# A hybrid decoder step on one core: norm and row sum links placed between masked maxima, and a rotation in four operations

## The reference

```python
h = rms_norm(x, norm_g); p = h @ w_in          # 1024 -> 3328 columns
# group A: 8 query heads, 2 key/value heads of 64, window 128
qa, ka = rotary(rms_norm(q), pos, 16, 5e5), rotary(rms_norm(k), pos, 16, 5e5)
s = einsum(q, k) * 64 ** -0.5; m = max(max(s + mask), sink)
prob = exp(s - m) / (sum(exp(s - m)) + exp(sink - m)); A = prob @ v
# group B: 4 retention heads of 128 with a decayed state
x = x + concat(silu(g_A) * A, silu(g_B) * B) @ w_out
```

## Time and profile before

| | |
|---|---|
| profiled execution, own time | 2014.24 us |
| its span | 2012.4 us |
| granted TensorE clock, mean | 0.978 |
| TensorE busy | 1858.1 us, 92% |
| VectorE busy | 1442.5 us, 72% |
| ScalarE busy | 712.0 us, 35% |
| block A's steps from 2 on, layer 0 | 97.4 to 422.7 us |
| block A's steps from 2 on, layer 1 | 1108.7 to 1400.7 us |
| a step, layer 0, from `L943` to `L943` | 23.2 (4 to 6), 21.4 to 21.8 (7 to 11), 20.3 (12), 19.0 (13), 19.1 (14), 17.8 and 18.7 us |
| a step, layer 1 | 19.9 to 20.3 (3 to 5), 19.1 to 19.5 (6 to 14), 18.0 and 18.4 us |

### The profile page before, as it was taken

One profiled execution on the slowest core, in us unless ns is written; L12 is line 12 of the kernel. 1 busy time (PEld: TensorE's weight loads), 2 busy tenths in 40 slices (PEclk: granted clock), 3 DMA queues, 4 the chain that ended last, 5 costly groups with the idle time before them and its releaser, 6 DMA issues.

```text
span 2012.4 us, 36841 instructions
## 1 busy us (share of the span) xinstructions
PE 1858.1 (92%) x12264; PEld 1047.5 (52%) x12264; DVE 1442.5 (72%) x4918; ACT 712.0 (35%) x1841; POOL 68.5 (3%) x108
## 2 busy tenths in 40 slices
PE   1778999997999999978998999999999999999999
PEld 0445555553555555543444655555555555555444
DVE  6679899976665666677885899999666657666542
ACT  4444565541232213232442455555213221232110
POOL 3010000010000000021001000001000000000000
PEclk9899999998999999999999999999999999999999
DMA  8332222032000210079994000001210021003864
GB/s 245 67 120 53 58 52 53 16 130 83 11 11 10 98 61 11 11 152 264 242 244 135 8 16 16 10 16 57 78 51 10 10 97 62 11 10 92 225 202 143
DMA packets 203403, 163.03 MB, mean 81 GB/s; under 512 B 145073, under 2 KB 175985, under 8 KB 203153
## 3 DMA queue, kind: packets, MB, share of 16 engines
q1 hardware_dynamic: 193584, 126.33, 23.2%
q0 software_dynamic: 9728, 35.66, 5.4%
HBM read 88.75 MB, written 41.16 MB: 65 GB/s over the span
## 4 chain that ended last, share of the span: by engine, by line
PE 60%; DVE 21%; ACT 4%; issue 4%; DMA 2%; SPq 1%; DVEq 0%; ACTq 0%
PE PA L499 24%; PE PB L499 24%; DVE r L1003 3%; ACT r L1564 2%; DVE r L979 2%; DVE mix L1043 2%; PE S L646 2%; PE OB L665 2%; PE TK L635 1%; PE S L681 1%; PE OB L672 1%; PE X L598 1%; DVE w_mx L834 1%; DMA r<-r 1%; DMA out<-land 1%
## 5 line engine op out<-in xcount | busy, mean ns | idle before, releaser
L499 PE MATMUL PA<-w_a,hT 128*128 128x512 f16 (+1 forms) x1920 | 405.2, 362 | 13.2 <-DVE land L957 13.2
L499 PE MATMUL PB<-w_a,hT 128*128 128x512 f16 (+1 forms) x1920 | 405.2, 362 | 0.0
L499 PEld LDWEIGHTS PA<-w_a,hT 128*128 (+1 forms) x1920 | 186.2, 99 | 187.5 <-DVE land L957 14.1
L499 PEld LDWEIGHTS PB<-w_a,hT 128*128 (+1 forms) x1920 | 185.8, 99 | 180.5 <-issue 11.8
L499 PE MATMUL PA<-w_b,hT 128*128 128x512 f16 x768 | 182.5, 389 | 16.8 <-DVE land L957 16.8
L499 PE MATMUL PA<-w_b,r 128*128 128x512 f16 x768 | 174.4, 384 | 19.4 <-DMA r<-r 17.1
L1564 ACT ACTIVATE r<-r,nm,unqk 128x256 f32<-128x256 f32 x256 | 150.5, 589 | 109.9 <-DVE sd L1011 109.9
L499 PE MATMUL PB<-w_b,hT 128*128 128x512 f16 x768 | 176.3, 379 | 0.0
L1622 ACT ACTIVATE r<-OB 128x128 f32<-128x128 f32 (+1 forms) x136 | 36.3, 272 | 389.8 <-PE S L681 362.4
L499 PE MATMUL PB<-w_b,r 128*128 128x512 f16 x768 | 171.3, 379 | 0.0
L1092 DVE TENSOR_TENSOR r<-S,t_dec 128x256 f32<-128x256 f32 x64 | 27.2, 425 | 154.4 <-PE S L646 154.2
(11 more groups left out here) (247 smaller groups left out, 2784.0 us busy)
## 6 DMA issues: line engine op xcount, KB each, us to landing
out<-r SPq DMA_DIRECT2D x40, 512.0 KB, 4.7
r<-mixed SPq DMA_DIRECT2D x32, 512.0 KB, 4.1
r<-in_x_prompt SPq DMA_DIRECT2D x25, 512.0 KB, 4.3
w_b<-in_w_in POOLq DMA_DIRECT2D x16, 512.0 KB, 9.0
mixed<-mix SPq DMA_DIRECT2D x32, 256.0 KB, 2.0
w_a<-in_w_in POOLq DMA_DIRECT2D x16, 512.0 KB, 8.6
mixed<-mix SPq DMA_DIRECT2D x64, 128.0 KB, 1.8
w_b<-in_w_out POOLq DMA_DIRECT2D x16, 512.0 KB, 7.5
```

The lines of the kernel that those rows point to most:

```text
L499: last = nc.tensor.matmul(out[0:s.rows, 0:n], lhs, w16(ph, k, p, wpart), start=(k == 0 and part == 0 and wpart == 0), stop=(k == KT - 1 an ...
```

## The change

It concerns VectorE's program of block A. `Chain` gets `put` (raise the semaphore) and `wait` apart. Steps 3 to 16 of each layer take a new order, written out in `a_tile`: the three row sum links of (u, 1) stand between the maxima of (t, 0); the norm links of tile s and the row sum links of (t, 0) stand between the maxima of (t, 1), the two lo parts of the probabilities of (t, 0) and the lo parts of weights. Both lo parts of weights are ahead of the rotation. In all steps the rotation multiplies both halves of the 16 channels by cos in one operation and by sin in another. No other engine's program changes.

```diff
+    def put(self, ins):
+    def wait(self):
...
             def a_rotate(L, s, ch):
...
-                V.tensor_tensor(rp1[0:r, :, 0, :], xa, cos, ALU.mult)
-                V.tensor_tensor(rp1[0:r, :, 1, :], xb, cos, ALU.mult)
-                V.tensor_tensor(rp2[0:r, :, 0, :], xa, sin, ALU.mult)
-                ch(V.tensor_tensor(rp2[0:r, :, 1, :], xb, sin, ALU.mult))
+                both = x[:, :, 0:ROT].rearrange("p h (c d) -> p h c d", c=2)
...
+                V.tensor_tensor(rp1[0:r, :, :, :], both, cos, ALU.mult)
+                ch(V.tensor_tensor(rp2[0:r, :, :, :], both, sin, ALU.mult))
...
                 def a_step(s, k=None):
+                    if not (s.fixed and s.c < 3):
+                        a_tile(s, k)
+                        return
...
+                def a_tile(s, k):
+
+                    t, u = s - 1, s - 2
+                    a_lo(L, t)
+                    a_land_q(L, s)
+                    a_plo(L, u, 1)
+                    old = a_rr(L, u, 1)
+                    alone(v, a_s, 2 * an(L, t) + 1)
+                    sm = Chain(v, ch_asp, 2, 2 * tn(L, t))
+                    a_rr_link(u, 1, old, 0)
+                    a_mask(t, 0, 0)
+                    a_rr_link(u, 1, old, 1)
+                    a_mask(t, 0, 1)
+                    a_rr_link(u, 1, old, 2)
+                    a_mask(t, 0, 2)
+                    sm.put(a_mask(t, 0, 3))
+                    a_least(sm, 0)
+                    a_sink(sm, 0)
+                    a_mix(L, u, 1, old)
+                    a_vcopy(L, t)
+                    ch = a_land_k(L, s)
+                    alone(v, a_s, 2 * an(L, t) + 2)
+                    sm = Chain(v, ch_asp, 2, 2 * tn(L, t) + 1)
+                    a_mask(t, 1, 0)
+                    a_norm_link(s, ch, 0)
+                    a_mask(t, 1, 1)
+                    a_norm_link(s, ch, 1)
+                    a_mask(t, 1, 2)
+                    a_norm_link(s, ch, 2)
+                    sm.put(a_mask(t, 1, 3))
+                    a_norm_link(s, ch, 3)
+                    a_least(sm, 1)
+                    a_norm_link(s, ch, 4)
+                    a_sink(sm, 1)
+                    new = a_rr(L, t, 0)
+                    a_rr_link(t, 0, new, 0)
+                    a_norm_link(s, ch, 5)
+                    a_rr_link(t, 0, new, 1)
+                    a_norm_link(s, ch, 6)
+                    a_plo_half(L, t, 0, 0)
+                    a_norm_link(s, ch, 7)
+                    a_rr_link(t, 0, new, 2)
+                    a_norm_link(s, ch, 8)
+                    a_plo_half(L, t, 0, 1)
+                    a_norm_link(s, ch, 9)
+                    if k is not None:
+                        w_low(L, "B0", k, 0)
+                    a_norm_link(s, ch, 10)
+                    if k is not None:
+                        w_low(L, "B0", k, 1)
+                    a_norm_link(s, ch, 11)
+                    a_rotate(L, s, ch)
+                    gate("A", L, s, 2, A_W, A_W + 2 * KV_W)
+                    a_mix(L, t, 0, new)
```

More of the change, by code:

```diff
@@ L182, in __call__ @@
     def __call__(self, ins):
+        self.put(ins)
+        self.wait()
+    def put(self, ins):
         self.n += 1
         ins.then_inc(self.sem, 1)
+    def wait(self):
         self.eng.wait_ge(self.sem, self.base + self.n)
@@ L1000, in a_softmax @@
                 else:
-                    m = t_ma[:, 2 if s.first else s.par, :].bitcast(BF16)
                     for h in range(A_GROUP):
[L1003 to L1008, removed]
@@ L1009, in a_softmax @@
[L1009 to L1023 removed]
+                        last = a_mask(s, g, h)
@@ new lines, in a_softmax, with a_mask @@
+                    ch.put(last)
+                    a_least(ch, g)
+                    a_sink(ch, g)
+                    return
+                ch.end()
+            def a_mask(s, g, h):
+                m = t_ma[:, 2 if s.first else s.par, :].bitcast(BF16)
+                return V.tensor_tensor_reduce(
+                    out=prob[:, h * 256:(h + 1) * 256], in0=SS[h // 2][:, (h % 2) * 256:(h % 2) * 256 + 256],
+                    in1=m, scale=1.0, scalar=-3e38, op0=ALU.add, op1=ALU.max,
+                    accum_out=mr[:, g, h:h + 1])
@@ new lines, in a_least, with a_sink @@
+            def a_least(ch, g):
+                ch.wait()
+                ch.put(V.scalar_tensor_tensor(out=nm[:, g, :], in0=mr[:, g, :], scalar=unqk[:, 1:2],
+                                              in1=nsk[:, g * A_GROUP:(g + 1) * A_GROUP], op0=ALU.mult, op1=ALU.min))
+            def a_sink(ch, g):
+                ch.wait()
+                V.tensor_tensor(sd[:, g, :], nm[:, g, :], sk[:, g * A_GROUP:(g + 1) * A_GROUP],
+                                ALU.add).then_inc(a_sm, 1)
+                ch.end()
@@ new lines, in a_rr, with a_rr_link @@
+            def a_rr(L, s, g):
+                n = 2 * an(L, s) + g
+                v.wait_ge(a_ex, n + 1)
+                return Chain(v, ch_amx, 3, n)
+            def a_rr_link(s, g, ch, i):
+                w = 1 if s.sample else A_GROUP
+                if i == 0:
+                    ch.put(V.tensor_tensor(rr[:, g, 0:w], rsum[:, g, 0:w], es[:, g, 0:w], ALU.add))
+                elif i == 1:
+                    ch.wait()
+                    ch.put(V.reciprocal(rr[:, g, 0:w], rr[:, g, 0:w]))
+                else:
+                    ch.wait()
+                    back = cs["A"][:, 1:2] if s.sample else cs["A"][:, 3:4]
+                    ch.put(V.tensor_scalar(rr[:, g, 0:w], rr[:, g, 0:w], back, None, ALU.mult))
@@ L1024, in a_mix @@
+            def a_mix(L, s, g, ch=None):
+                n, b = 2 * an(L, s) + g, s.par
+                if ch is None:
+                    ch = a_rr(L, s, g)
+                    for i in range(3):
+                        a_rr_link(s, g, ch, i)
+                ch.wait()
                 v.wait_ge(a_pv, n + 1)
```

54 lines of the change are left out of this document (39 added, 15 removed).

## The result

The changed kernel takes 2068.6 us in the median (2066.4 to 2070.9), the kernel before on the same chip 2012.8: a ratio of 1.028, interval 1.0254 to 1.0297. It is slower, as forecast, but by 56 us where 27 stood in the forecast, and 2068.6 lies above the range.

The account below looks back on a forecast made before the run. VectorE was taken to set the pace. Step terms of 11.0, 2.4, 4.0, 3.0 and 4.5 us sum to 25, plus 2 for one clock fall: 2014.2 + 27 = 2041 us, range 2024 to 2062.

Parts of the forecast that it names:

- the fall that it added: One drop of TensorE's granted clock to its lower level behind a wait, put at 2 us in all.
- loaded steps: Layer 0's steps 3 to 12, layer 1's 3 to 6: VectorE's extra work delays first scores; +3 and +4.5 us in all.
- terms of 0.3 and of 0.9 to 1.3 us a step: Ten loaded steps lose 0.3 us each; four where VectorE already waited for the scores lose 0.9 to 1.3.
- Spacing: VectorE's small links cost 0.08 us instead of 0.20 between longer operations, rotation products 0.24 each; 2.0 us less work per step.
- The rival that links are held: A placed VectorE link waits for the operation before it, costing 0.17 us, not 0.08: 25 us more, 2066; chance 0.06.
- Place: VectorE reaches group 1's first maximum before TensorE's scores land: a new wait of 2.6 us, with the norm links queued behind.
- The tail: VectorE, group 1's first maximum to rotation's end: from 5.14 to 7.73 us with weights, from 5.0 to 6.52 without.
- two lo parts of weights 0.66 each: Term of the tail: VectorE's two lo parts, moved ahead of the rotation, add 0.66 us each, 1.32 together.
- The clock: TensorE's clock falls to 1.2 of 2.4 GHz after waits, costing 1.7 us; one fall, 2 us, was added.
- plain step: Layer 1's steps 7 to 14, layer 0's 13 and 14: TensorE waits only at the transposes; 19.4 to 20.9 us in layer 1.
- The rival of the clock: The new 2 us wait brings TensorE's clock down in most plain steps: 20 us more, 2061; chance 0.06.

Follow-up runs that it names:

- norm chain back: Changed kernel with both lo parts of weights at their old places and the norm chain whole and chained ahead of group 1's first maximum: 1994.7 us, 0.9918.
- The filler: Changed kernel, TensorE's loops written out, with ten unread matmuls ahead of the transposes in steps 8 to 15: 2058.1 us, repeated at 2060.0 us.
- first weight back: Changed kernel with only the first lo part of weights back ahead of the landing of k, the second still in the tail: 2024.8 us, 1.006.
- high part last: Changed kernel with the second lo part of weights back behind the mix and ScalarE's second high part moved behind the tanh: 2028.3 us, 1.0068.
- second weight back: Changed kernel with only the second lo part of weights back behind the mix, the first still in the tail: 2053.4 us, 1.0212.
- the control: Changed kernel with TensorE's loop over steps written out as for the filler, but no extra matmul: 2072.2 us, 1.0291.

## Why the prediction was right about the direction and wrong about the size

The intervals between transposes on TensorE, before and after, part by part:

| steps | before | after | grown | forecast |
|---|---|---|---|---|
| layer 1, 3 to 6 | 79.6 | 81.5 | 1.9 | 1.2 |
| layer 1, 7 to 14 | 156.1 | 186.6 | 30.5 | 11.0 |
| layer 1, 15 and 16 | 37.0 | 40.7 | 3.7 | 2.0 |
| layer 0, 3 to 6 | 90.8 | 92.4 | 1.6 | 2.4 |
| layer 0, 7 to 12 | 129.7 | 140.1 | 10.3 | 3.8 |
| layer 0, 13 and 14 | 38.8 | 46.3 | 7.5 | 2.4 |
| layer 0, 15 and 16 | 37.1 | 39.1 | 2.0 | 2.0 |

The sum is 57.5 us; the forecast's column gives 24.8, its 25, without the fall that it added. (The split of the forecast over the loaded steps is worked out afterwards, from its terms of 0.3 and of 0.9 to 1.3 us a step, with two of the latter in each of layer 0's rows.) Two of the forecast's terms do not follow from its own step times: steps 13 and 14 of layer 0 at 20.8 are 2.8 above their 38.8 together and not 2.4, and steps 15 and 16 at 19.7 are 2.4 above their 37 in each layer and not 2.0. That is 1 us in all and decides nothing.

- *Spacing*: right. Links 0.07 to 0.08 us behind their neighbour, products 0.24 apart. The rival that links are held is out. By the Trainium skill, "VectorE: DVE Perf Modes", section "The DRAIN you can't avoid", `L838` at 1334.47 would have had to wait for the end of `L1073` at 1334.56; it starts 0.09 sooner. The section itself sends the reader on to the one on two instructions without a wait between them for an operation that isn't held, and the forecast left that out when it weighed the rule; the rows side with that second section.
- *Place*: right. 2.88 us of waiting at the first maximum for 2.6. With norm chain and links the other way round, nothing else changed, the wait is gone and 30 us come back ("norm chain back").
- *The tail*: right by its own terms, 7.73 + 1.10 = 8.83 with weights and 6.43 for 6.52 without. **The step that failed** is "two lo parts of weights 0.66 each": the two instructions were costed as VectorE's time alone. Their place also sets when ScalarE may go on. The forecast asked what is queued behind VectorE's wait, but not who waits for the two lo parts. In layer 1 that is 1.10 x 8 = 8.8 us, in layer 0 6.2 us, in the waits shown above; moved alone, the two parts cost 36 us, and the forecast's own terms for them (1.32 a step with weights, 16 of these) give 21.
- *The clock*: right in kind, and right in the price of a fall in a plain step, 1.7 us. **The term that was mis-sized** is their number: one was added, and layer 1 has seven in a row behind waits of 3.2 to 3.3 us. The forecast's wait was 2 us; the 1.1 us from ScalarE carried it on to 3.2, where nearly every step falls. So the two errors are one behind the other. Six of the falls lengthen steps 7 to 14 of layer 1: 11.0 as forecast, 8.8 for ScalarE, 6 x 1.7 = 10.2 for the falls, together 30.0 for 30.5 measured. The step without a fall is 22.1 us, the 20.9 of the forecast and 1.1. The seventh fall is in the row of steps 15 and 16.
- Layer 0's rows are argued the same way (two falls in steps 13 and 14, 3.4 us, and 0.8 us of waiting each), but no experiment changes layer 0 alone. The filler bears out the falls of steps 13 and 14, with 1.7 and 1.5 us given back; in steps 7 to 12, 10.3 us for 3.8, how the rest divides between waits and falls stays open.
- *The rival of the clock* gave 2061 and had 0.06. The forecast set against it that the clock fell behind only "a few" of layer 0's eleven waits. By the trace that it had it was more than that: of the six waits of 1.6 to 2.1 us two were followed by a fall, and of the three of 3.0 to 4.3 us two. Two in six of twelve plain steps are four falls, 7 us where it added 2. And it did not ask at which length of its own wait the rival would decide. Two of those six in the kernel before, the four microseconds from the scores on, behind a wait of 2.06 us and behind one of 1.88:

```profile
242.88:246.88 4.00, 3.80 (x52) 2.70 (x53) 3.96 (x13) 0.62 (x2) 0.00 (x0) 1.00 0.00 0
264.27:268.27 4.00, 4.00 (x41) 3.10 (x42) 3.96 (x13) 0.63 (x2) 0.00 (x0) 0.63 1.14 243
```

## What to carry to other kernels

Placing links of a chain between long operations does hide them, at 0.07 us instead of 0.20. For the norm links it paid, by some 4 us, where these operations stand ahead of the wait that sets the step, and cost 30 us where they stand behind it, since the chain then no longer fills that wait. A wait is the best place for a chain: ask what covers the wait now before moving the cover. For each instruction that is moved, list who waits for its semaphore and what stands in that engine's queue behind the waiting instruction; here an instruction of 0.7 us had five microseconds of ScalarE hanging on it.

## What the runs showed of the chip that I had not expected

The length of a wait alone does not say whether the clock falls behind it. Behind waits of 1.4 to 1.8 us at layer 1's transposes there was no fall in two versions ("first weight back", "high part last") and there were three in eight in a third ("second weight back"). At 2.5 us it was four in eight, and 2.48 fell where 2.54 did not; at 2.7 to 2.8 us, in layer 0 after the change, five in eight. At 3.2 to 3.6 us it was seven in eight. The one that was spared there had the longest wait, 3.56; in the control it was one of 3.31, and in the repeat of the changed kernel none was. The runs show no rule for which is spared. A fall in a plain step cost 1.7 us and lengthened the loop by as much; in layer 0's step 8 the control with a fall and the filler run without one both take 23.8 us. The Trainium skill, "TensorE: Matmul & The Clock Gate", section "HAM oscillation — how this bites in real kernels", tells of a wait in every turn of a loop after which each turn starts at the lower clock and pays again; layer 1 after the change agrees, with 0.57 in the first 4 us behind the wait, though here the wait is for another engine and not for a transfer. Work that nobody reads, put into such a wait, made the kernel 12 us faster than its control.
